# Sample keys of the sparse-attention layer: turned by VectorE in 32x32 blocks, scored on sixteen 32x32 tiles

## What is computed

```python
s2 = jnp.einsum('bqhgd,bqhkrd->bqhgkr', qr_blk, k_b) * ATTN_SCALE    # selected blocks of past keys
s2 = jnp.where(valid[:, :, :, None], s2, -jnp.inf)
p2 = jax.nn.softmax(s2.reshape(sh[:4] + (-1,)), axis=-1).reshape(sh)
o_sel = jnp.einsum('bqhgkr,bqhkrd->bqhgd', p2, v_b)
o_win = band_attention(q_rot, kw_all, vw_all, w_off, C_WIN)          # the same with 512 window keys
```

## Time and profile before

| | |
|---|---|
| median of 3 runs | 2064.89 us (2061.18 to 2072.67) |
| span of the profiled execution | 2066.1 us |
| PE busy | 1915.6 us, 93% |
| DVE busy | 1063.6 us, 51% |
| ACT busy | 833.9 us, 40% |
| POOL busy | 1.4 us |
| instructions | 43255 |

### The profile page before, as it was taken

One profiled execution on the slowest core, in us unless ns is written; L12 is line 12 of the kernel. 1 busy time (PEld: TensorE's weight loads), 2 busy tenths in 40 slices (PEclk: granted clock), 3 DMA queues, 4 the chain that ended last, 5 costly groups with the idle time before them and its releaser, 6 DMA issues.

```text
span 2066.1 us, 43255 instructions
## 1 busy us (share of the span) xinstructions
PE 1915.6 (93%) x16603; PEld 1621.0 (78%) x16603; DVE 1063.6 (51%) x1777; ACT 833.9 (40%) x1761; POOL 1.4 (0%) x8
## 2 busy tenths in 40 slices
PE   4999999999999899998999997899999777879998
PEld 3899999888888799798999995444444467769998
DVE  3358777666443544346689665433333322235454
ACT  2344444554344333445755552333323322234454
POOL 0000000000000000000000000000000000000000
PEclk9999999999999799999999999999999899999999
DMA  5788878633877488576555552244444389885454
GB/s 192 232 269 263 263 257 265 206 113 123 267 263 247 146 280 272 203 233 202 157 151 162 162 155 75 92 139 132 136 130 136 116 286 295 286 280 188 170 179 139
DMA packets 306536, 406.05 MB, mean 197 GB/s; under 512 B 18472, under 2 KB 222823, under 8 KB 305088
## 3 DMA queue, kind: packets, MB, share of 16 engines
q1 hardware_dynamic: 306384, 403.94, 61.3%
HBM read 391.43 MB, written 12.45 MB: 195 GB/s over the span
## 4 chain that ended last, share of the span: by engine, by line
PE 77%; DVE 11%; SPq 4%; DMA 3%; issue 2%; ACT 2%; DVEq 0%; ACTq 0%
PE PJ L1541 44%; PE XB L1993 8%; PE XB L1567 4%; PE XB L2004 4%; DVE w_low L980 2%; SPq L490 2%; DVE scr L999 2%; SPq L496 1%; PE XB L1813 1%; PE PJ L1981 1%; PE XB L1656 1%; DMA cring<-in_cache_c_win_kv_dram 1%; PE PJ L1960 1%; PE XB L1585 1%; PE XB L2063 1%
## 5 line engine op out<-in xcount | busy, mean ns | idle before, releaser
L1541 PE MATMUL PJ<-xh,w_up 128*128 128x264 f32 x3072 | 920.2, 300 | 40.1 <-DVE w_low L980 21.5
L1541 PE MATMUL PJ<-xl,w_up 128*128 128x264 f32 x3072 | 881.0, 287 | 0.0
L1541 PE MATMUL PJ<-xh,w_low 128*128 128x264 f32 x3072 | 879.3, 286 | 0.0
L980 DVE TENSOR_TENSOR w_low<-wring,w_up 128x512 fp32r<-128x512 f32 x768 | 524.8, 691 | 606.0 <-ACT w_up L602 595.6
L602 ACT CAST w_up<-wring 128x512 fp32r<-128x512 f32 x768 | 473.3, 619 | 644.7 <-PE PJ L1541 536.9
L1541 PEld LDWEIGHTS PJ<-xh,w_up 128*128 128x128 f32 x3072 | 587.6, 191 | 79.8 <-issue 56.4
L1541 PEld LDWEIGHTS PJ<-xl,w_up 128*128 128x128 f32 x3072 | 587.7, 191 | 1.4
L1541 PEld LDWEIGHTS PJ<-xh,w_low 128*128 128x128 f32 x3072 | 585.6, 191 | 0.0
L1993 PE MATMUL XB<-wring,proj 128*32 128x512 f32 x320 | 167.1, 605 | 1.1 <-DVE proj L1419 0.9
L2004 PEld LDWEIGHTS XB<-const,cring 128*128 128x128 f32 x640 | 70.8, 141 | 86.1 <-ACT wring L926 41.9
L1412 DVE COPY wring<-XB 128x512 f32<-128x512 f32 x80 | 55.3, 691 | 159.6 <-PE XB L2004 159.6
(11 more groups left out here) (301 smaller groups left out, 1448.7 us busy)
## 6 DMA issues: line engine op xcount, KB each, us to landing
wring<-in_w_in_ab_dram SPq DMA_DIRECT2D x144, 512.0 KB, 4.6
cring<-in_cache_c_cmp_kv_dram SPq DMA_DIRECT2D x128, 512.0 KB, 3.9
cring<-in_cache_c_sel_kv_dram SPq DMA_DIRECT2D x256, 256.0 KB, 2.9
wring<-in_w_in_c_dram SPq DMA_DIRECT2D x112, 512.0 KB, 3.7
wring<-in_w_ple_gate_dram SPq DMA_DIRECT2D x64, 512.0 KB, 3.6
cring<-in_cache_a_kv_dram SPq DMA_DIRECT2D x48, 512.0 KB, 5.0
wring<-in_w_out_ab_dram SPq DMA_DIRECT2D x32, 512.0 KB, 5.2
cring<-in_cache_c_win_kv_dram SPq DMA_DIRECT2D x64, 256.0 KB, 4.1
```

Source lines behind the costliest of these rows:

```text
L980: nc.vector.tensor_tensor(w_low[:, e % NE], raw(e), w_up[:, e % NE].bitcast(F32), ALU.subtract).then_inc(sem("w_lo"), 1)
L1541: ins = nc.tensor.matmul(PJ[(2 * bl + c) % 4][:, 0:T], w[:, e % NE, k, tileT(c)], x[:, kx, :], start=(kx == 0 and w is w_up and x is xh), ...
```

## The change

Keys are turned by VectorE in blocks of 32x32, straight from the ring to SBUF (`KTs`), a page of 128x512 at a time; TensorE no longer transposes them, and ScalarE and VectorE no longer copy them out of PSUM. A block holds 32 dimensions (db) of 32 keys (kb) of a head, so the scores are now made with 32 rows and 32 columns of the array: for each set 64 float32 matmuls with a moving operand of 4 times 32 columns, in the order db, kb, h. Row group kb writes PSUM bank XB[kb], head h its 32 partitions, so sixteen consecutive matmuls go to sixteen different tiles. The queries therefore have to stand on all four partition groups for each db: GpSimd clears two areas of 2048 numbers per partition, and ScalarE makes 16 copies of 32 partitions between unit 0's exponentials and the loop (`q_copies`).

In the loop `k_sets(u)` gives whole sets to an iteration: 40 sets over 29 iterations, so 18 iterations have one and 11 have two. On VectorE two pages are turned between `cu_probs(u + 1)` and `cu_scores(u + 2)`, the rest after it. On TensorE all of an iteration's sets stand at its end; nothing stands between `cu_probs(u)` and `cu_values(u)`. The window's sets come first, the cache's after them. Scores are taken in four pieces, one for each bank. Other tiles only change their place in SBUF.

```diff
-            for k in steps:                                  # VectorE; ScalarE the same for even k
-                if k % 2 == 1:
-                    dve.wait_ge(sem("kt_T"), 8 + k + 1)
-                    nc.vector.tensor_copy(KTc[:, k % CH, :], XB[1 + k % 3][:, :]).then_inc(sem("kt_odd"), 1)
+            for pg in pages:
+                n, q = pg // WT, pg % WT
+                if q == 0:
+                    dve.wait_ge(sem(f"set_in{n % 2}"), 64 * (n // 2 + 1))
+                    if n >= 2:
+                        dve.wait_ge(sem("kt_used"), n - 1)
+                nc.vector.transpose(KTs[n % 2][:, q, :], hring[:, 4 * (n % 2) + q, :]).then_inc(sem("kt_T"), 1)
+                if q == WT - 1 and n == B:
+                    take_window()
+                elif q == WT - 1 and n % B == 0 and n > B:
+                    take_scores(n // B - 2)
...
             for u in range(32):                              # VectorE
-                k_odd(before)
+                sets = k_sets(u)
+                pages = range(WT * sets.start, WT * sets.stop)
                 if u + 1 < 32:
                     cu_probs(u + 1)
-                k_odd(after[:2])
+                key_pages(pages[:2])
                 if u + 2 < 32:
                     cu_scores(u + 2)
-                k_odd(after[2:])
+                key_pages(pages[2:])
...
+            def key_scores(n):                               # TensorE
+                pe.wait_ge(sem("kt_T"), 8 + WT * n + WT)
...
+                for db in range(4):
+                    for kb in range(4):
+                        rows = slice(32 * kb, 32 * kb + 32)
+                        for h in range(CH):
+                            ins = nc.tensor.matmul(XB[kb][32 * h:32 * h + 32, tileT(at)].rearrange("p (g j) -> p g j", g=WT),
+                                                   q_block(db)[rows, b, h, :], KTs[n % 2][rows, :, P * h + 32 * db:P * h + 32 * db + 32],
+                                                   start=(n in (0, B) and db == 0), stop=(b == B - 1 and db == 3),
+                                                   skip_group_check=True)
+                ins.then_inc(sem("kt_used"), 1)
...
                 cu_probs(u)                                  # TensorE
-                keys(before)
                 cu_values(u)
                 if u + 2 < 32:
                     cu_scores(u + 2)
-                keys(after)
+                for n in k_sets(u):
+                    key_scores(n)
...
+            pool.wait_ge(sem("c_out"), 16 * 18)              # GpSimd
+            nc.gpsimd.memset(q_rows[0], 0.0).then_inc(sem("q_zero"), 1)
+            pool.wait_ge(*done("scmp_made"))
+            nc.gpsimd.memset(q_rows[1], 0.0).then_inc(sem("q_zero"), 1)
...
+            def q_copies():                                  # ScalarE, once, ahead of the loop
+                act.wait_ge(sem("q_zero"), 2)
+                for db in range(4):
+                    src = proj[32 * db:32 * db + 32, 40:56, S:T].rearrange("p (h g) b -> p b h g", h=CH)
+                    for kb in range(4):
+                        nc.scalar.copy(q_diagonal(db)[32 * kb:32 * kb + 32], src).then_inc(sem("q_rows"), 1)
...
-            link(nc.vector.memset(Q[:, 0:1024], 0.0))        # VectorE, ahead of the loop
-            for b in range(B):
-                ins = nc.vector.tensor_copy(qzr[:, b, :, 4 * b:4 * b + 4], proj[:, 40:56, S + b].rearrange("p (h g) -> p h g", h=CH))
```

More of the change, by code:

```diff
@@ L291, in hybrid_trunk, with k_sets @@
         vnew = KV[:, 768:896]
[L295 to L299, removed]
+        K_SETS, K_FROM = 5 * B, 3
+        def k_sets(u):
+            lo, hi = ((u + n - K_FROM) * K_SETS // (32 - K_FROM) for n in range(2))
+            return range(lo, hi) if u >= K_FROM else range(0)
         s_new = cols(2)
@@ L930, in _ @@
             nc.scalar.copy(P_sum, XB[0][:, 128:256]).then_inc(sem("psum_taken"), 1)
+            q_copies()
             for u in range(32):
@@ L1414, in take_scores, with key_pages @@
-            def take_scores(c):
[L1416 to L1427, removed]
+            def key_pages(pages):
+                for pg in pages:
[9 more added lines that the diff above has]
+                        take_scores(n // B - 2)
@@ new lines, in take_window @@
+            def take_window():
+                dve.wait_ge(sem("kt_used"), B)
+                for kb in range(4):
+                    ins = nc.vector.tensor_copy(S_win.rearrange("p (w s j) -> p w s j", w=WT, s=4)[:, :, kb, :],
+                                                XB[kb][:, 0:P].rearrange("p (w j) -> p w j", w=WT))
+                link(ins)
+                dve.sem_inc(sem("win_taken"), 1)
+                link(nc.vector.tensor_reduce(cmx[:, 4:5], S_win, AX, ALU.max))
+            def take_scores(c):
+                dve.wait_ge(sem("kt_used"), B * (c + 2))
+                own = S_sel[:, 512 * c:512 * c + 512]
+                for kb in range(4):
+                    neg = sneg[:, 8 * c:8 * c + 8].rearrange("p (g o) -> p g o", o=2)[:, :, kb // 2:kb // 2 + 1]
+                    ins = nc.vector.tensor_tensor(own.rearrange("p (g s j) -> p g s j", g=4, s=4)[:, :, kb, :],
+                                                  XB[kb][:, tileT(c)].rearrange("p (g j) -> p g j", g=4),
+                                                  over(neg, [P, 4, 32]), ALU.add)
+                link(ins)
+                dve.sem_inc(sem("S_taken"), 1)
+                link(nc.vector.tensor_reduce(cmx[:, c:c + 1], own, AX, ALU.max))
@@ L1983, in cu_values @@
                 ins.then_inc(sem("cu_o"), 1)
[L1988 to L2007 removed]
+            def key_scores(n):
+                pe.wait_ge(sem("kt_T"), 8 + WT * n + WT)
+                if n == 0:
+                    pe.wait_ge(sem("q_rows"), 16)
+                if n == B:
+                    pe.wait_ge(sem("win_taken"), 1)
+                elif n % B == 0 and n > B:
+                    pe.wait_ge(sem("S_taken"), n // B - 1)
+                at, b = max(n // B - 1, 0), n % B
+                for db in range(4):
+                    for kb in range(4):
+                        rows = slice(32 * kb, 32 * kb + 32)
[5 more added lines that the diff above has]
+                ins.then_inc(sem("kt_used"), 1)
             pe.wait_ge(*done("pc_p"))
@@ L2022, in _ @@
                     pe.wait_ge(sem("ptexp_taken"), 1)
-                before, after = k_steps(u)
                 cu_probs(u)
-                keys(before)
                 cu_values(u)
@@ L2033, in _ @@
                       .then_inc(step("imp_made"), 1)
-            key_scores(K_STEPS - 1)
             pe.wait_ge(sem("cu_o_taken"), 32)
```

84 lines of the change are left out of this document (29 added, 55 removed).

## The result

The changed kernel takes 2095.53 us (median of 4 runs, 2093.47 to 2098.0), the kernel before 2065.71 (4 runs, the three shown and 2066.53). The ratio is 1.0147, 95% interval 1.0124 to 1.0171: 1.5% slower. The profiled execution took 2098.0 us, its span is 2096.2, which is 30.1 more than before.

What follows compares the result with a forecast made beforehand. TensorE alone was taken to bound the stage, 314.4 us. Afterwards a serial chain, 122, pages 80 + 30 and TensorE 46 + 6 make 284, -30; others +3: span 2039, forecast 2038 us, range 2014 to 2102.

Steps and rivals of the forecast that it cites:

- the chain: Each of 29 iterations, probabilities to keys through four engines: steps in series, nothing overlapping, 4.20 us mean without the pages.
- the page: VectorE turning one 128x512 page: taken as 0.69 us, between bounds of 0.486 and 1.22; 160 pages, 80 + 30 us.
- the takings: Scores taken in four pieces: each of four times holds TensorE about 1 us, before about 0.6; +1.5 us.
- so issue is not what sets 26 ns, the stream in each tile is: TensorE's small matmuls: four pairs start within about 20 ns on different tiles, so streaming sets the 26 ns per pair.
- P = 1.6: TensorE's time in us for one set of 64 matmuls, between 1.1 at full clock and 2.1 at half; 46 us.
- P = 2.5: Time in us of a set on TensorE, 19 ns per pair, above which the kernel would be slower than before.
- they are hidden, with 0.6 to spare: TensorE's values and scores end near 3.9 us, before VectorE reaches its scores near 4.5, so they add nothing.
- 0.2 more on the chain: Added per iteration for a TensorE clock between full and half: 29 x 0.2 = 6 us.
- Rival (a): Row groups not beside each other, or pairs not issued that fast 128 in a row: set 3.4 us, 2098 us; chance 0.20.
- Rival (b): TensorE's clock at its lower level all through the stage: set 2.1 us, 2059 us, no change seen; chance 0.12.
- (c): A page on VectorE costs near the upper bound, 1.22 us: +85 us, 2123 us; chance 0.10.
- (d): Rival (a) and Rival (b) together: a set takes 6.8 us, 2239 us; chance 0.05.

## Why the prediction was wrong

Forecast 2038 us, measured 2095.53, slower where faster was the likeliest. The stage was to take 284 us and took 336.7. By the table of means above, the steps from the probabilities to the first keys are 14 us of these 52.7 (18 x 0.71 + 11 x 0.15), the last set of each iteration 39 (18 x 1.01 + 11 x 1.89), and the pages between two sets gave 1 back. The query copies, +3 in the forecast, cost 7.

**Right: the chain.** TensorE's probabilities, ScalarE's copies and exponentials, VectorE's probabilities, two pages, scores, two pages, keys: all in series, as the earlier trace rows were added up. (One term is added up wrong: 1405.69 to 1407.10 are 1.41 us, not 1.35. It makes no difference to the result.) An even unit was to take 3.89 + 2.76 + 0.26 = 6.91 us up to its keys and took 6.72. **Right: the page**, T = 0.69 from a neighbour of its width; 0.68 alone, 0.61 to 0.65 in a row of two or four. **Right: the takings**, some 4 us, **GpSimd's memset** of 1.80 us, hidden, and the loads, which held up VectorE 5.7 us in all.

**Failed: "so issue is not what sets 26 ns, the stream in each tile is", and with it P = 1.6.** The tiles do stream beside each other. But from four pairs that start within 20 ns I took a pair to cost nothing of its own, and wrote only one latency. A set of 128 pairs takes 0.6 to 0.7 us more than that (2.75 against 8 x 0.213 + 0.42 = 2.12, 1.83 against 1.12). P is 2.75 us at the lower clock level (forecast 2.1) and 1.83 at the full one (forecast 1.1). Over the 18 single iterations it is 2.61 in the mean: 18 x 1.0 = 18 us. The prediction's own point of decision, P = 2.5, did not hold: the measured sets lie near it, where the sum had no change, and the kernel is 30 us slower, because other terms were too small as well.

"In iterations with two sets the first P hides behind the four pages of the second" was right: the second set's keys start 2.66 us after the first's, as the pages do (2.76 forecast). But the second set then takes 3.49 us in the mean where the forecast had 1.6: 11 x 1.9 = 21 us. About half of that is the price of a set as above, and about half are the holes of the last section, which the forecast did not have.

**Failed: "they are hidden, with 0.6 to spare", and "0.2 more on the chain" for the clock.** The 0.6 was worked out at full clock. At the lower level TensorE's values and scores are late in odd units, 18.3 us in all; the odd unit shown was to take 7.41 us up to its keys and took 8.33, of which 1.31 are this wait. The prediction saw that the clock would fall and gave it 29 x 0.2 = 6 us beside the half step in P. By the run with idle matmuls, which brings it back only to 0.84, it was worth at least 30. These shares overlap (the clock is part of P), so they are not to be added.

**Failed: q_copies, +3.** I took ScalarE's 0.25 us copy of 16 partitions and let them overlap. A copy of 32 partitions by 128 out of a strided source takes 0.416 us, and none overlaps: 7.0.

**The rivals.** Rival (a) gave 2098 us, close to the time measured, and that is luck: its row groups do run beside each other, and without a hole no set took its P of 3.4. That pairs cannot be issued at that rate 128 in a row was right as far as the means go. The floor of about 25 ns from start to start that the Trainium skill gives ("TensorE: Matmul & The Clock Gate", section "Wait — 56ns, not 53.3ns?") does not hold across tiles here: the second 64 pairs start 13 ns apart at the full clock, 21 at the lower. The Trainium skill has, on the same page, section "Measured speedup vs the span model", about 4 ns of issue for each tile, from one matmul on each; the trace, with eight pairs on each tile, has about 7 over the streaming. Rival (b), the clock alone, was real, but beside the price of the pairs, not in its place. Rivals (c) and (d) did not happen. So the error lay in terms mis-sized together, the set, the clock and the wait for scores, all of them on a chain with no slack that is run through 29 times.

## What to carry to other kernels

Work taken off a busy engine may have been the cover of a chain: add up the chain that is left, at the clock that the engine will be granted when it waits, and look for a second stream to put between its dependent steps. Here the same change, with its consumer one iteration behind its producer, the producer's pages ahead of unrelated work, loads page by page and the copies moved, goes from 1.5% slower to 4.7% faster. Small matmuls on many tiles have a price by the pair besides the stream; a burst of four does not show it.

## What the runs showed that I had not expected

- The second 64 pairs of a set on sixteen tiles start 13 ns apart at the full clock and 21 at the lower, about 7 ns over the streaming, in either order of the tiles and with either width. They come in bursts with pauses. What sets this is not shown.
- Adding seven idle matmuls to each iteration saves 30 us: the granted clock in the stage goes from 0.60 to 0.84.
- Some sets have a hole in which TensorE waits for nothing that the profile shows. A row of the changed kernel's timeline, then the sums of such waits, 1310 to 1640 us, with half the columns and with half the matmuls:

```profile
1412.54 0.40 PEld L2033 LDWEIGHTS XB<-wring,kcmp 32*32 32x32 f32 x33 [1.03 <-issue]
```

```profile
PEld XB L2033 <- issue: 11.2, 10, 1.9
```

```profile
PEld XB L2033 <- issue: 0.2, 1, 0.2
```

  The changed kernel has nine of them, 10.4 us, each in or just ahead of the second set of an iteration with two, and one of 1.1 us behind another such set, ahead of L1999. So ten of the eleven iterations with two sets have one. With half the columns they stay, with half the matmuls they are gone. So they go with the number of instructions, not with what these stream. The page has 137 packets of instructions on one queue where the page of before had 105 and that of half the matmuls 117. That the instructions came late fits this, but no run shows it.
